# First half first in the last products, and four pieces of the memory's keys and values beside the norms

## The chip, the cores and the metric

The kernel runs on one core of a Trainium2 chip. The metric is device time in microseconds for one launch: the median of three runs, each of which carries out the whole computation once. A separate execution was recorded by the hardware profiler, and all rows of a trace come from it.

## What is computed

Two layers of a decoder trunk, 256 tokens of 1024 values, all float32. The two places that matter here are the norms and the cross-attention to a memory that does not depend on x:

```python
def layer(x, mem_n, l):                       # cut from the reference
    p = rmsnorm(x, norm_mix[l]) @ w_in[l]     # one projection, columns for four mixers
    y = concat(hgrn2(p), gated_deltanet(p), rglru(p), rwkv7(p))
    x = x + y @ w_out[l]
    h = rmsnorm(x, norm_xattn[l])
    q = h @ xattn_wq[l]
    k = mem_n @ xattn_wk[l]                   # mem_n = rmsnorm(mem), 256 tokens
    v = mem_n @ xattn_wv[l]
    x = x + softmax(q k^T / 16) v @ xattn_wo[l]      # 4 heads
    h = rmsnorm(x, norm of the FFN)
    return x + (swiglu(h) if l == 0 else top2_of_8_experts(h))
```

A final rmsnorm ends it. The delta-rule mixers (gated DeltaNet and RWKV-7) need the inverse of unit lower triangular 64x64 blocks; HGRN2 is computed in levels of doubling block size.

## The kernel before, in words

The kernel is written engine by engine: each of SyncE (SP), TensorE (PE), ScalarE (ACT) and VectorE (DVE) has its own program, and semaphores named by strings order them.

**Weights.** All large weights come in chunks of 1 MB. `plan_chunks` writes down their order, and SP issues the loads in that order (L384) into a ring of three buffers `raw`. Load d waits until the buffer of load d-3 has been read: for an ordinary chunk that is the semaphore `w_lo`, for a piece of memory weights `kv_done`. An ordinary chunk is split in two: ScalarE copies it to `whi` in a rounded format (`ahead`, L447), VectorE subtracts and writes `wlo` (`ahead`, L871). There are three pairs of split buffers; the split of chunk n waits for `chunk_done` of chunk n-3.

**Products.** Each product with x runs in three passes, high by high, low by high, high by low. A product whose output has its columns in the partitions (w_in, w_q, gate, up) takes one chunk as 48 matmuls of 128x256 (`cm_product`, L1554). A product that is added to x (w_out, w_o, the FFN's down) is summed over its chunks in four banks of PSUM, two for the first 128 tokens and two for the second; a chunk is 24 matmuls of 128x512 (`tm_product` calls `tm_part`, L1574). `tm_phase` runs four such chunks. In every chunk before the change both halves of the tokens are worked through together, pass by pass, and the semaphore `chunk_done` is raised at the end of the chunk.

**A norm.** Behind the last chunk VectorE first splits the chunks that are due (`ahead` in `tm_add`, L909), waits for `chunk_done`, and adds the four banks to x (L858). ScalarE and VectorE then make the sums of squares and the reciprocal roots, token half by token half; VectorE writes a diagonal matrix of them (L861). TensorE's `norm(i)` (L1590) multiplies x by that diagonal, which both scales and transposes it: the **turn** of x, 16 matmuls of 128x128 in fp32, 32 instructions in the trace. ScalarE and VectorE copy the result out as high and low parts, and `first_product` (L1610) takes the first chunk of the next phase, whose k-steps follow those copies. There are five norms with such a sum before them: attention and FFN in layer 0, mixer, attention and experts in layer 1.

**Memory keys and values.** For each layer there are eight **pieces**, four of `xattn_wk` and four of `xattn_wv`, each one chunk of 1 MB and 16 fp32 matmuls straight from `raw` (32 instructions, helper line L1539), in one bank (`KV_BANK`). They depend on nothing but the memory and are used at the attention alone, so they are laid between the small matmuls of the mixers. `kv(l, i, ks)` (L1614) runs the k-steps `ks` of piece i, two matmuls for each of eight k-steps; when all eight are done it raises `kv_done`, and ScalarE's `kv_put` (L486) copies the bank to `kT` or `vA` and raises `kv_put`. Before the change both layers have the same plan: pieces 0 to 3 among the levels of HGRN2 (`hgrn`, L1728), piece 4 and the two halves of piece 5 in the inverse of DeltaNet (`inverse`, L1818, called from `deltanet`, L1865), piece 6 step by step in DeltaNet's recurrence, piece 7 in `rwkv` (L1912).

**The inverse** multiplies 64x64 blocks level by level; VectorE masks each level's blocks (L858) before TensorE goes on.

## Time and profile before

| what | value |
|---|---|
| three runs | 1994.59, 1995.18, 1998.88 us |
| median | 1995.18 us |
| profiled execution | 1995.15 us, span in the trace 1993.3 us |
| TensorE busy | 1870.8 us, 94% of the span |
| VectorE busy | 1467.0 us, 74% |
| ScalarE busy | 1131.4 us, 57% |
| DMA | 465.99 MB, mean 234 GB/s |

The span is what lies between the first and the last recorded instruction; the device time holds 1.85 us more. "Busy" counts an engine's instructions that compute; a bracket such as [4.39 <-DVE TMP L861] at the end of a row gives the idle time of the engine ahead of it and what ended that. Order of the program: layer 0's mixers to 308 us, its attention to 384, its FFN to 581, layer 1's mixers to 878, its attention to about 954, then the experts. PEclk is the clock granted to TensorE as a share of the full 2.4 GHz, so 0.50 is 1.2 GHz.

### The profile page before, as it was taken

The numbers are of one execution on the slowest core, as the hardware profiler recorded it, in microseconds if no ns is written. First come the engines' busy times: TensorE is split into PE (matmuls) and PEld (weight loads), VectorE is DVE, ScalarE is ACT, GpSimd is POOL, SyncE is SP. The second block draws the span as 40 slices with busy tenths as digits, with TensorE's granted clock in tenths as the row PEclk, the third lists the DMA queues.
The fourth block names the chain that finished last, engine by engine and source line by source line (L and its number), as shares of the span: only waits on it lengthen the run. The fifth ranks groups of instructions, "written<-read, shape, count | busy, mean of one in ns | idle before, by whom it ended". The sixth has DMA issues, their size and how long they took to land.

```text
span 1993.3 us, 29711 instructions
## 1 busy us (share of the span) xinstructions
PE 1870.8 (94%) x12520; PEld 1614.1 (81%) x12521; DVE 1467.0 (74%) x1547; ACT 1131.4 (57%) x1065; POOL 0.2 (0%) x4
## 2 busy tenths in 40 slices
PE   7998799899999988899699999999999999999996
PEld 6976688799989877778588888888888888888885
DVE  6767645444457676554688989989899898998985
ACT  5555224443344652144377767777677777777774
POOL 0000000000000000000000000000000000000000
PEclk9998899999999999899899999999999999999998
DMA  7541004255545421023499999989999999999992
GB/s 238 170 148 61 27 23 162 85 188 182 183 146 169 157 78 44 23 85 106 171 334 345 379 345 366 369 335 380 341 371 365 332 382 343 371 365 335 370 377 99
DMA packets 239450, 465.99 MB, mean 234 GB/s; under 512 B 11856, under 2 KB 87760, under 8 KB 239312
## 3 DMA queue, kind: packets, MB, share of 16 engines
q1 hardware_dynamic: 239312, 464.03, 65.6%
q8 instruction: 101, 1.65, 0.3%
q14 instruction: 37, 0.30, 0.0%
HBM read 462.95 MB, written 1.05 MB: 233 GB/s over the span
## 4 chain that ended last, share of the span: by engine, by line
PE 85%; DVE 9%; ACT 3%; issue 2%; DMA 1%; DVEq 0%; SPq 0%; ACTq 0%
PE ps L2062 31%; PE ps L1554 15%; PE ps L2072 15%; PE ps L1539 11%; PE ps L1574 7%; DVE MT L858 4%; PE ps L2118 1%; ACT MT L438 1%; PE ps L2093 1%; PE ps L1610 1%; DVE MT L861 1%; PE ps L2133 1%; DVE MT L864 1%; DVE TMP L858 1%; ACT TMP L438 1%
## 5 line engine op out<-in xcount | busy, mean ns | idle before, releaser
L1315 DVE TENSOR_TENSOR wlo<-raw,whi 128x2048 fp32r<-128x2048 f32 x140 | 320.4, 2291 | 55.8 <-ACT whi L736 55.5
L736 ACT ACTIVATE whi<-raw 128x2048 fp32r<-128x2048 f32 x140 | 268.9, 1922 | 120.9 <-PE ps L2072 71.3
L871 DVE TENSOR_TENSOR wlo<-raw,whi 128x2048 fp32r<-128x2048 f32 x85 | 194.5, 2289 | 98.9 <-ACT whi L447 98.8
L1315 DVE TENSOR_TENSOR wlo<-PT,whi 128x2048 fp32r<-128x2048 f32 x84 | 192.1, 2291 | 31.3 <-ACT whi L736 30.1
L447 ACT ACTIVATE whi<-raw 128x2048 fp32r<-128x2048 f32 x85 | 162.1, 1907 | 45.3 <-PE ps L1574 43.6
L2062 PE MATMUL ps<-whi,hE_hi 128*128 128x512 f32 x672 | 185.4, 398 | 2.4 <-DVE hE_lo L1384 2.4
L736 ACT ACTIVATE whi<-PT 128x2048 fp32r<-128x2048 f32 x84 | 161.4, 1922 | 35.0 <-PE ps L2062 34.2
L2062 PE MATMUL ps<-wlo,hE_hi 128*128 128x512 f32 x672 | 180.1, 390 | 0.0
L2062 PE MATMUL ps<-whi,hE_lo 128*128 128x512 f32 x672 | 179.8, 389 | 0.0
L2062 PEld LDWEIGHTS ps<-wlo,hE_hi 128*128 128x128 f32 x672 | 126.2, 188 | 27.2
L2062 PEld LDWEIGHTS ps<-whi,hE_lo 128*128 128x128 f32 x672 | 126.1, 188 | 26.7
L2062 PEld LDWEIGHTS ps<-whi,hE_hi 128*128 128x128 f32 x672 | 122.0, 188 | 24.8 <-DVE hE_lo L1384 2.6
L2072 PE MATMUL ps<-whi,act_hi 128*128 128x512 f32 x336 | 130.8, 389 | 1.4 <-DVE act_lo L1359 1.4
L2072 PE MATMUL ps<-whi,act_lo 128*128 128x512 f32 x336 | 130.8, 389 | 0.0
L2072 PE MATMUL ps<-wlo,act_hi 128*128 128x512 f32 x336 | 130.7, 389 | 0.0
L1539 PE MATMUL ps<-MT 64*64 64x64 f32 (+1 forms) x2528 | 99.3, 233 | 26.5 <-DVE MT L858 19.2
L1539 PEld LDWEIGHTS ps<-MT 64*64 64x64 f32 (+1 forms) x2528 | 90.6, 145 | 38.7 <-issue 19.4
L1554 PE MATMUL ps<-hT_hi,whi 128*128 128x256 f32 x848 | 119.7, 284 | 0.0
L1554 PE MATMUL ps<-hT_hi,wlo 128*128 128x256 f32 x848 | 119.0, 283 | 0.0
L1554 PE MATMUL ps<-hT_lo,whi 128*128 128x256 f32 x848 | 119.0, 283 | 0.0
L858 DVE TENSOR_TENSOR MT<-MT,ps 128x256 f32<-128x256 f32 (+2 forms) x99 | 44.6, 450 | 90.0 <-PE ps L1554 75.5
L1554 PEld LDWEIGHTS ps<-hT_hi,whi 128*128 128x128 f32 x848 | 109.9, 192 | 0.9
(272 smaller groups left out, 3391.1 us busy)
## 6 DMA issues: line engine op xcount, KB each, us to landing
raw<-in_moe_w_up SPq DMA_DIRECT2D x111, 1024.0 KB, 7.2
PT<-in_moe_w_down SPq DMA_DIRECT2D x56, 1024.0 KB, 6.6
PT<-in_moe_w_gate SPq DMA_DIRECT2D x55, 1024.0 KB, 6.9
TMP<-in_moe_w_gate SPq DMA_DIRECT2D x55, 1024.0 KB, 7.0
raw<-in_moe_w_down SPq DMA_DIRECT2D x55, 1024.0 KB, 6.3
raw<-in_w_in SPq DMA_DIRECT2D x28, 1024.0 KB, 5.4
raw<-in_ffn_w_gate SPq DMA_DIRECT2D x11, 1024.0 KB, 5.4
raw<-in_ffn_w_up SPq DMA_DIRECT2D x11, 1024.0 KB, 5.5
```

The lines of the kernel that those rows point to most:

```text
L438: return chain.link(lambda: nc.scalar.activation(o, i, f, **kw))
L447: nc.scalar.activation(whi[i % SPL][:, :], raw[d % RAW][:, :], ACT.Copy).then_inc(S("w_hi"), 1)
L736: nc.scalar.activation(ex_hi[m % XSPL], ex_raw[m % XRAW], ACT.Copy).then_inc(S("w_hi"), 1)
L858: return chain.link(lambda: V.tensor_tensor(o, x0, x1, op))
L861: return chain.link(lambda: V.tensor_scalar(o, x0, s1, s2, op0, op1) if op1 else V.tensor_scalar(o, x0, s1, None, op0))
L871: V.tensor_tensor(wlo[i % SPL][:, :], raw[d % RAW][:, :], whi[i % SPL][:, :].bitcast(F32), ALU.subtract).then_inc(S("w_lo"), 1)
L1315: V.tensor_tensor(ex_lo[m % XSPL], ex_raw[m % XRAW], ex_hi[m % XSPL].bitcast(F32), ALU.subtract).then_inc(S("w_lo"), 1)
L1539: return Signalled(pe.matmul(o, lhsT, rhs, start=start, stop=stop, skip_group_check=True))
L1554: ins = pe.matmul(ps[:, bank, SEQ * m:SEQ * m + SEQ], wp[a_][:, k, P * m:P * m + P], src[b_][:, k, :], start=i == 0 and k == 0, stop=last)
L1574: ins = pe.matmul(ps[:, 4 + 2 * t + hf, :], src(b_, kk, t), wp[a_][:, kk, 512 * hf:512 * hf + 512], start=first and kk == 0 and i == 0, st ...
L2062: ins = pe.matmul(ps[:, bank, :], h_[b_][:, X_K * i + k, :], wp[a_][:, k, :], start=i == 0 and n_ == 0 and k == 0, stop=i == 1 and n_ == 2 ...
L2072: ins = pe.matmul(ps[:, 4 + hf, :], act_[b_][:, P * (TM_ROWS * i + kk):P * (TM_ROWS * i + kk) + P], wp[a_][:, kk, 512 * hf:512 * hf + 512] ...
```

## The change

Two things are done.

**The last output chunk** of w_out, w_o and down is worked through by a new function `tm_last`: all 12 matmuls for the first 128 tokens, semaphore `tm_half`, then the 12 for the second, `chunk_done`. VectorE's `tm_add` waits for `tm_half` ahead of the two sums of the first tokens, and for `chunk_done` ahead of the other two. It is used at all five places.

**Four pieces move to norms.** With PRE = 3, six matmuls of a piece (three k-steps) stand ahead of the turn and the other ten behind it. The pieces are: piece 7 of layer 0 at the attention norm of layer 0; piece 0 of layer 1 (now a piece of `xattn_wv`) at the FFN norm; piece 1 of layer 1 (`xattn_wk`) at layer 1's mixer norm; piece 7 of layer 1 at its attention norm. What was piece 5 leaves the inverse in both layers, and the later ones move up by one. In the levels of layer 1 only two pieces are left, one ahead of them and one in quarters in four levels. The loads stand in SP's queue where the pieces stand, and ScalarE's copies move with them.

```diff
+PIECES = [[("xattn_wk", j) for j in range(4)] + [("xattn_wv", j) for j in range(4)],
+          [("xattn_wv", 0)] + [("xattn_wk", j) for j in range(4)] + [("xattn_wv", j) for j in range(1, 4)]]
...
+        if layer:
+            out += pieces[1][1:2]
         out += [("cm", "w_in", layer, c) for c in W_IN_COLS]
         out += [("tm", "w_out", layer, TM_ROWS * j) for j in range(3)]
-        out += [("kv", "xattn_wk", layer, c) for c in range(0, D, CM_COLS)]
-        out += [("kv", "xattn_wv", layer, c) for c in range(0, D, CM_COLS)]
+        out += pieces[layer][2 * layer:7]
         out += [("tm", "w_out", layer, 3 * TM_ROWS)]
+        out += pieces[layer][7:]
         out += [("cm", "xattn_wq", layer, c) for c in range(0, D, CM_COLS)]
         out += [("tm", "xattn_wo", layer, r) for r in range(0, KT, TM_ROWS)]
         if layer == 0:
+            out += pieces[1][:1]
...
-        KV_BANK = [7, 5, 6, 7, 6, 7, 7, 2]
+        KV_BANK = [[7, 5, 6, 7, 6, 7, 2, 1], [3, 1, 7, 7, 6, 7, 2, 3]]
+        PRE = 3
...
-            def tm_add(n0, count, ahead_to):
+            def tm_add(k, n0, count, ahead_to):
                 ahead(ahead_to)
-                dve.wait_ge(S("chunk_done"), n0 + count)
                 for t in range(TT):
+                    if t:
+                        dve.wait_ge(S("chunk_done"), n0 + count)
+                    else:
+                        dve.wait_ge(S("tm_half"), k)
                     for hf in range(2):
...
+            def tm_last(n, src):
+                pe.wait_ge(S("w_lo"), n + 1)
+                for t in range(TT):
+                    for kk in range(TM_ROWS):
+                        ins = tm_part(n, src, False, True, kk, t)
+                    ins.then_inc(S("chunk_done" if t else "tm_half"), 1)
...
                     if v == 1:
                         pe.wait_ge(S("gd_gd"), l + 1)
+                    if l:
+                        if v == 2:
+                            pe.wait_ge(S("kv_put"), 2 * NH + 3)
+                        if 2 <= v < LEVELS - 1:
+                            kv(1, 3, range(2 * v - 4, 2 * v - 2))
+                        continue
...
-                    if v == 0:
-                        pe.wait_ge(S("y_put"), 4 * l + 2)
-                    if v < 2:
-                        kv(l, 5, range(KT // 2 * v, KT // 2 * v + KT // 2))
...
             def attention(l):
+                kv(l, 7, range(PRE))
                 pe.wait_ge(S("x_done"), 6 * l + 2)
                 norm(2 + 3 * l)
+                kv(l, 7, range(PRE, KT))
...
             def swiglu():
+                kv(1, 0, range(PRE))
                 pe.wait_ge(S("x_done"), 4)
                 norm(3)
+                kv(1, 0, range(PRE, KT))
...
             for l in range(DEPTH):
+                if l:
+                    kv(1, 1, range(PRE))
                 norm(norm_index(l))
+                if l:
+                    kv(1, 1, range(PRE, KT))
                 cm_phase(first_chunk["w_in", l], 14, norm_index(l), lambda j: gates_ahead(l, j))
```

Three places show how instructions move. (A row is a line of the code, the operation, output<-input, the tile and a count; line numbers of the changed kernel differ.) The first is TensorE at the attention norm of layer 0. Before:

```order
L1574 MATMUL ps<-wlo,hT_hi 128x512
L1574 MATMUL ps<-whi,hT_lo 128x512
L1539 MATMUL ps<-TMP,x 128x128 x16
L1610 MATMUL ps<-hT_hi,whi 128x256 x16
L1610 MATMUL ps<-hT_hi,wlo 128x256 x16
L1610 MATMUL ps<-hT_lo,whi 128x256 x16
L1554 MATMUL ps<-hT_hi,whi 128x256 x8
```

Changed:

```order
L1589 MATMUL ps<-whi,hT_lo 128x512
L1554 MATMUL ps<-raw,memT 128x256 x6
L1554 MATMUL ps<-TMP,x 128x128 x16
L1554 MATMUL ps<-raw,memT 128x256 x10
L1634 MATMUL ps<-hT_hi,whi 128x256 x16
L1634 MATMUL ps<-hT_hi,wlo 128x256 x16
L1634 MATMUL ps<-hT_lo,whi 128x256 x16
L1569 MATMUL ps<-hT_hi,whi 128x256 x8
```

The turn (`ps<-TMP,x`) has six matmuls of a piece ahead of it and ten behind it, where it stood between the two products.

The second is SP's queue from the end of the FFN to layer 1, with what each load waits for. Before:

```order
L384 DMA raw<-in_ffn_w_gate 128x8x256 [waits w_lo]
L384 DMA raw<-in_ffn_w_up 128x8x256 [waits w_lo]
L384 DMA raw<-in_ffn_w_down 128x2x1024 [waits w_lo] x2
L384 DMA raw<-in_w_in 128x8x256 [waits w_lo] x14
L384 DMA raw<-in_w_out 128x2x1024 [waits w_lo]
```

Changed:

```order
L393 DMA raw<-in_ffn_w_up 128x8x256 [waits w_lo]
L393 DMA raw<-in_ffn_w_down 128x2x1024 [waits w_lo] x2
L393 DMA raw<-in_xattn_wk 128x8x256 [waits w_lo]
L393 DMA raw<-in_w_in 128x8x256 [waits w_lo] x2
L393 DMA raw<-in_w_in 128x8x256 [waits kv_done]
L393 DMA raw<-in_w_in 128x8x256 [waits w_lo] x11
L393 DMA raw<-in_w_out 128x2x1024 [waits w_lo]
```

A piece stands ahead of the first w_in chunk, so each w_in chunk takes the buffer that is released one load later than before: the second waits for the split of the last FFN chunk, and the third for the piece to be done.

The third is TensorE in DeltaNet's inverse in layer 0 (`MT` is the blocks, `PT` and `con` the operands of RWKV's preparation between them). Before:

```order
L1539 MATMUL ps<-PT 128x128 x8
L1539 MATMUL ps<-raw,memT 128x256 x16
L1539 MATMUL ps<-con,MT 64x64 x16
L1539 MATMUL ps<-raw,memT 128x256 x8
L1539 MATMUL ps<-MT 64x64 x48
L1539 MATMUL ps<-PT,con 128x512
L1539 MATMUL ps<-raw,memT 128x256 x8
```

Changed:

```order
L1554 MATMUL ps<-PT 128x128 x8
L1554 MATMUL ps<-raw,memT 128x256 x16
L1554 MATMUL ps<-con,MT 64x64 x16
L1554 MATMUL ps<-MT 64x64 x48
L1554 MATMUL ps<-PT,con 128x512
L1554 MATMUL ps<-MT 64x64 x208
```

Both groups of eight piece matmuls are gone from it; the whole piece ahead of it stays.

## Rows read from the trace of the kernel before

**Rows 1.** Page, header: span
```profile
span 1993.3 us, 29711 instructions
```

**Rows 2.** Windows: stretch, PE PEld DVE ACT POOL busy (count), PEclk, DMA share, GB/s
```profile
696.00:722.90 26.90, 26.90 (x309) 21.98 (x310) 23.13 (x48) 9.98 (x18) 0.00 (x0) 1.00 0.36 118
985.00:1993.00 1008.00, 987.12 (x4587) 820.59 (x4585) 880.14 (x601) 718.03 (x531) 0.00 (x0) 0.99 0.94 344
```

**Rows 3.** Timeline, PE, layer 1, around the attention norm
```profile
877.87 0.39 PE L1574 MATMUL ps<-whi,hT_lo 128*128 128x512 f32 x1
...
882.65 6.05 PE L1539 MATMUL ps<-TMP,x 128*128 128x128 f32 x32 [4.39 <-DVE TMP L861]
...
895.28 0.99 PE L1554 MATMUL ps<-hT_hi,whi 128*128 128x256 f32 x7
```

**Rows 4.** Timeline, DVE, the same place
```profile
866.36 2.29 DVE L871 TENSOR_TENSOR wlo<-raw,whi 128x2048 fp32r<-128x2048 f32 x1
...
874.87 2.29 DVE L871 TENSOR_TENSOR wlo<-raw,whi 128x2048 fp32r<-128x2048 f32 x1 [3.14 <-ACT whi L447]
878.30 2.85 DVE L858 TENSOR_TENSOR x<-x,ps 128x512 f32<-128x512 f32 x4 [1.14 <-PE ps L1574]
...
881.25 0.15 DVE L861 TENSOR_SCALAR st<-st 128x1 f32<-128x1 f32 x1
```

**Rows 5.** Timeline, PE, last product's last matmul and second product's start, three other norms
```profile
307.73 0.39 PE L1574 MATMUL ps<-whi,hT_lo 128*128 128x512 f32 x1
...
324.85 1.12 PE L1554 MATMUL ps<-hT_hi,whi 128*128 128x256 f32 x8
...
383.71 0.39 PE L1574 MATMUL ps<-whi,hT_lo 128*128 128x512 f32 x1
...
400.16 1.12 PE L1554 MATMUL ps<-hT_hi,whi 128*128 128x256 f32 x8
...
580.93 0.39 PE L1574 MATMUL ps<-whi,act_lo 128*128 128x512 f32 x1
...
597.95 1.09 PE L1635 MATMUL ps<-hT_hi,wsm_hi 128*8 128x256 f32 x8
```

**Rows 6.** Chain of waits: norm, product and memory piece at full clock
```profile
417.60 5.47 PE ps L1574 x24
...
600.90 5.75 PE ps L1554 x48
...
1054.13 3.57 PE ps L2118 x32
```

**Rows 7.** Timeline, PE, one memory piece
```profile
742.15 7.17 PE L1539 MATMUL ps<-raw,memT 128*128 128x256 f32 x32
```

**Rows 8.** Windows at 1 us, start of two norms: PEclk is the third number from the end
```profile
312.00:313.00 1.00, 0.50 (x2) 0.53 (x3) 0.75 (x4) 0.95 (x4) 0.00 (x0) 0.50 0.96 398
388.00:389.00 1.00, 0.51 (x4) 0.55 (x5) 0.76 (x4) 0.95 (x4) 0.00 (x0) 1.00 0.00 0
```

**Rows 9.** Timeline, DVE, inverse's third level in layer 0 and in layer 1
```profile
196.08 0.95 DVE L858 TENSOR_TENSOR MT<-ps,con16b 128x256 f32<-128x256 f32 x2 [2.33 <-PE ps L1539]
...
764.07 0.95 DVE L858 TENSOR_TENSOR MT<-ps,con16b 128x256 f32<-128x256 f32 x2 [0.82 <-PE ps L1539]
```

**Rows 10.** DMA issues: queue, count, size, median us from issue to landing
```profile
raw<-in_w_in SPq DMA_DIRECT2D x28, 1024.0 KB, 5.4
...
raw<-in_xattn_wq SPq DMA_DIRECT2D x8, 1024.0 KB, 5.1
```

**Rows 11.** Timeline, split of the last FFN chunk (DVE) and of the second w_in chunk
```profile
571.11 2.28 DVE L871 TENSOR_TENSOR wlo<-raw,whi 128x2048 fp32r<-128x2048 f32 x1
...
575.98 1.92 ACT L447 ACTIVATE whi<-raw 128x2048 fp32r<-128x2048 f32 x1 [0.89 <-PE ps L1574]
```

**Rows 12.** Timeline, PE: an idle time of 2.71 us and the clock behind it
```profile
115.06 0.66 PE L1542 MATMUL ps<-con,PT 128*128 128x128 f32 x4 [2.71 <-ACT MT L438]
```

**Rows 13.** Windows, the same place
```profile
115.97:119.20 3.23, 3.23 (x9) 2.56 (x8) 0.00 (x0) 3.01 (x9) 0.00 (x0) 0.50 0.89 308
```

More of the change, by code:

```diff
@@ L498, in gates_ahead @@
                     mem_norm(j)
+                if l and j == 1:
+                    kv_put(1, 1)
                 if j == 6:
@@ L583, in hgrn @@
                         a(tmp(1), ps[:, 4, :], ACT.Copy).then_inc(S("hg_v"), 1)
-                    if v % 2 == 0 and v < LEVELS - 1:
-                        kv_put(l, v // 2)
+                    if v % 2 == 0 and v < LEVELS - 1 - 4 * l:
+                        kv_put(l, v // 2 + 2 * l)
                     rglru(l, v)
@@ L659, in deltanet @@
                 head_rms(l, 1, 0)
-                kv_put(l, 6)
+                kv_put(l, 5)
             def rwkv(l):
@@ L1523, in _ @@
                 split_small(l + 1)
-                tm_add(first_chunk["w_out", l], 4, first_chunk["xattn_wq", l] + 2)
+                tm_add(3 * l + 1, first_chunk["w_out", l], 4, first_chunk["xattn_wq", l] + 2)
                 attention(l)
@@ L1584, in tm_product @@
                 ins.then_inc(S("chunk_done"), 1)
+            def tm_last(n, src):
[4 more added lines that the diff above has]
+                    ins.then_inc(S("chunk_done" if t else "tm_half"), 1)
             def tm_phase(n0, src, done=0):
-                for j in range(done, 4):
-                    tm_product(n0 + j, lambda b_, kk, t: src[b_][:, TM_ROWS * j + kk, P * t:P * t + P], j == 0, j == 3)
+                for j in range(done, 3):
+                    tm_product(n0 + j, lambda b_, kk, t: src[b_][:, TM_ROWS * j + kk, P * t:P * t + P], j == 0, False)
+                tm_last(n0 + 3, lambda b_, kk, t: src[b_][:, TM_ROWS * 3 + kk, P * t:P * t + P])
             def norm(i):
@@ L1649, in gates_ahead @@
                     small_product(7, l).then_inc(S("ab_mm"), 1)
+                if l and j == 3:
+                    pe.wait_ge(S("kv_put"), 2 * NH + 2)
                 if j == 2:
@@ L1737, in hgrn @@
                 pe.wait_ge(S("sm_ready"), 2 * (l + 1))
-                kv(l, 0, range(KT))
+                kv(l, 2 * l, range(KT))
                 pe.wait_ge(S("s_kA"), l + 1)
@@ L1746, in hgrn @@
                 mm(ps[:, 6, 8:16], ones, g8).then_inc(S("gd_cum"), 1)
-                kv(l, 1, range(KT // 2))
+                if l == 0:
+                    kv(0, 1, range(KT // 2))
                 for v in range(LEVELS):
```

71 lines of the change are left out of this document (39 added, 32 removed).

## The prediction

> **What bounds the kernel now.** I first read the header of the page, a span of 1993.3 us [rows 1]. The windows then split it. From 985 us on the experts run for 1008 us with TensorE busy 987.12 us [rows 2]; the change touches nothing there, so everything is decided in the first 985 us, where TensorE waits at few places. One kind is the turn of x at each norm. In layer 1 the last output product's last matmul ends at 877.87 + 0.39 = 878.26, TensorE idles 4.39 us for the sums, the statistics and the diagonal that VectorE and ScalarE make, the turn takes 6.05 us, and the first product is done when the second starts, at 895.28 [rows 3]: 17.02 us from the last product's end. The same stretch is 324.85 - 308.12 = 16.73 us at the attention norm of layer 0, 400.16 - 384.10 = 16.06 us at the FFN norm and 597.95 - 581.32 = 16.63 us at the mixer norm of layer 1 [rows 5]. The other kind is the mixers, chains of small matmuls and VectorE work. In the chunkwise levels of layer 1 TensorE is busy 26.90 us of 26.90, but VectorE is busy 23.13 us in 48 instructions there [rows 2], and the whole idle time of 3.77 us is at most 0.08 us an instruction plus one larger stall: both engines are full, and a piece taken from TensorE alone shows up only where VectorE really waited.
>
> My base is the profiled execution, 1995.15 us (its span and 1.85 us around it). The median of the three runs is 1995.18, so the two agree.
>
> **Part 1, pieces leave the mixers.** A piece is 16 matmuls, 32 TensorE instructions, 7.17 us at full clock [rows 7], 0.224 us an instruction; four pieces are 28.7 us. In both layers the two halves of piece 5 leave the delta rule's inverse. Behind the first half VectorE has no wait; behind the second it stood 2.33 us in layer 0 and 0.82 us in layer 1 for TensorE, ahead of the third level's mask [rows 9]. The blocks that it waits for then need only X, which VectorE itself had just made, so I take back 2.3 and 0.8 us: **-3.1 us**. In the levels of layer 1 two pieces' worth leaves (16 of the 24 steps). Bounds: nothing, if VectorE carries those levels, and 3.8 us, if all its idle time were due to TensorE [rows 2]. I take 0, since 3.77 us over 48 instructions is what dependent instructions leave between them.
>
> **Part 2, the sums start earlier.** The last output chunk now does all 12 matmuls of its first 128 tokens first. A chunk is 24 matmuls in 5.47 us [rows 6], so the first half is ready 5.47 / 2 = 2.7 us before the second. But VectorE splits the next phase's second chunk just ahead of the sums: that split began at 874.87 and ended at 877.16, 1.1 us before the product's end [rows 4]. So the sums start at most 1.1 us earlier where that split stays where it is. From the start of the sums to the turn it is 4.35 us (878.30 to 882.65) [rows 3, 4]: 2.85 for four sums, then the statistics of the first tokens, from 881.25 to the turn, 1.4 us. At the experts' norm the code leaves no chunk to split ahead of the sums; there the first pair of sums is done before the product ends, and the second pair, half of 2.85 = 1.43 us, still waits for its end. The turn starts 1.43 + 1.4 + 0.1 for handing over = 2.9 us behind the product instead of 4.39: **-1.5 us**, passed on whole, since the router is a chain.
>
> **Part 3, a piece enters each of four turns.** Six matmuls (12 x 0.224 = 2.7 us) run before the turn, in idle time, ten (4.5 us) behind it. Three things pay. The idle time hides the six. A turn at full clock costs 3.57 us, as 32 matmuls of the same shape do in the experts, not 6.05 [rows 3, 6]: the clock stood at 0.50 (1.2 GHz) when the attention turn of layer 0 began and at 1.00 (2.4 GHz) when the FFN turn began [rows 8], each after 4.4 us of idle time. And the first product runs without stalls, 5.75 us [rows 6], because the high and low parts that it waited for are written under the ten. So a stretch is now (start of the turn) + 3.57 + 4.5 + 5.75 = start + 13.8 us. The start hangs on the loads. SP's queue is in order and a ring of three buffers is shared, so a piece put into the queue moves the loads behind it by one release:
> - FFN norm: the two chunks split before the sums are loaded in time; the sums start 1.1 us ahead of the product's end, the turn 3.25 us behind it. 3.25 + 13.8 = 17.05 against 16.06: **+1.0 us**.
> - Attention norms: the second w_q chunk now takes the buffer that the last w_out chunk frees at 866.36 + 2.29 = 868.65 [rows 4]. With 5.1 us to land [rows 10] it is there at 873.75, copied (1.92) at 875.7 and subtracted (2.29) at 878.0, 0.26 us before the product's end. Turn at +4.1: 17.9 against 17.02 and 16.73: **+0.9 and +1.2 us**.
> - Mixer norm of layer 1: the second w_in chunk waits for the split of the last FFN chunk, which ends at 571.11 + 2.28 = 573.39; so far it had landed before ScalarE wanted it at 575.98 [rows 11]. With 5.1 us it lands at 578.5, is copied at 580.4 and subtracted at 582.7, 1.4 us behind the product's end. The sums, behind it on VectorE, start later than now although they wait for less: turn at +5.8, 19.6 against 16.63: **+3.0 us**. The landing is 5.1 us in one row and 5.4 in the other, which gives +3.0 to +3.3.
>
> At this last turn TensorE idles 5.8 - 2.7 = 3.1 us behind the six matmuls. An idle time of 2.71 us was followed by a clock of 0.50 for 3.2 us [rows 12, 13]. I take the clock to fall here too. Bounds: 0 if it holds, 6.05 - 3.57 = 2.5 us for a whole turn at half clock; the fall comes some time after the idle time began, so **+2.0 us**.
>
> The Trainium skill, "DMA: Bandwidth & Descriptors", sections "Anatomy of one DMA" and "Where 436 GB/s comes from", gives about 2.0 us of fixed cost and 436 GB/s. For 1 MB that is an estimate of 4.4 us instead of the 5.1 measured; with it the second chunks of the two attention norms and of the mixer norm would be there 0.7 us earlier each, and the sum below would be 2.1 us smaller. The trace has the duration, so it decides.
>
> **What costs nothing.** The late loads behind a piece (third w_q, w_in or gate chunk, released when the piece is done) land some 5 us after it, about as the first product ends, and are wanted a product (5.75 us) later: 2 us of slack are left after the split. ScalarE's four copies of pieces (0.6 us each) move to places where it waits for TensorE. The banks that the pieces use are wanted only two or three products later. If this cover went, each late chunk would cost its lateness, 1 us or so.
>
> **Sum.** -3.1 - 1.5 + 1.0 + 0.9 + 1.2 + 3.0 + 2.0 = +3.5 us: 1995.15 + 3.5 = **1998.6 us**. About 0.2% (4 us) is what a measurement of this kernel can tell from no change; the forecast lies inside it, near its slow edge (1999.2).
>
> **The rivals.**
> - *The clock falls at the attention turns and in the inverses too (slower).* TensorE idles 4.1 - 2.7 = 1.4 us in those turns, and in the inverses it loses 7.2 us of work each. If the clock falls behind idle time that short too, two turns cost 2.5 us more each: 1998.6 + 5.0 = 2003.6. It decides from where the clock has fallen before the turn begins. Against it: the falls in my rows stand behind 2.7 us [rows 12, 13] and 4.4 us [rows 3, 8] of idle time. With the late loads each a little later it also covers the upper part of the range. Chance of this and of like losses that reach over 1999.2: 0.29.
> - *The clock holds at the mixer turn (same).* The FFN turn began at 1.00 after 4.4 us of idle time [rows 8], so a wait of that length does not always bring the clock down. 1998.6 - 2.0 = 1996.6; if it holds at the experts' turn as well, up to 2.5 us less: 1994.1. Chance 0.22. The Trainium skill, "TensorE: Matmul & The Clock Gate", section "HAM oscillation", says that a wait between groups of matmuls sends the next group to the slow clock. By that rule alone the fall is sure; rows 8 show that it is not at every wait of this length.
> - *The change does what its parts promise (faster).* If the loads land before they are wanted, the sums start 2.7 us early at all turns, the turn at +2.9: 2.9 + 13.8 = 16.7 in each, which is +0.6, 0, +0.1 and -0.3 instead of +1.0, +1.2, +3.0 and +0.9, and no clock falls: 1998.6 - 5.7 - 2.0 = 1990.9. Against it stands the split ahead of the sums [rows 4], which no load can move. Together with the 3.8 us of the levels it would be 1987. Chance, with a part of that gain alone counted in: 0.15.
> - The forecast itself, with its own spread of 2 us: 0.34.
>
> **The numbers.** The forecast and the second rival lie within 0.2% (0.55, which leaves 0.01 of the forecast's spread above it). Slower by over 0.2%: 0.29 + 0.01 = 0.30. Faster: 0.15. The range leaves out about 1 in 10 on each side: from 1991.5, close above the promise, to 2002.8, just short of the first rival.
>
> **What would show it.** In the changed kernel's timeline the turn of layer 1's mixer norm starts 5 to 6 us behind the last product, with the sums released by the split of the second w_in chunk, not by TensorE; the attention turns start at about +4.1, the FFN turn at +3.25, the experts' at +2.9; 32 turn instructions take 3.6 us at three turns; VectorE's wait ahead of the inverse's third level is gone, while the stretch of the levels in layer 1 is as long as before. I am wrong if the mixer turn starts at +3, if the levels of layer 1 are shorter by over 1 us, or if the clock is 0.50 in the attention turns.

## The result and the profile after

The changed kernel takes 2002.20 us (median of 7 runs, 2000.60 to 2002.73), the kernel before 1996.35 (7 runs, 1994.59 to 1998.88): ratio 1.0029, 95% interval 1.0020 to 1.0038, so 5.9 us or 0.29% slower. The forecast was 1998.6 us with a range of 1991.5 to 2002.8. The forecast added 3.5 us to its base and 5.9 us were measured; the range held the time. The likeliest case (within 0.2%, chance 0.55) did not come, the smaller one (slower by over 0.2%, chance 0.30) did.

The header and part 1 of the changed kernel's page. The profiled execution took 2000.60 us:

```profile
span 1998.8 us, 29714 instructions
...
PE 1870.5 (94%) x12520; PEld 1615.1 (81%) x12521; DVE 1466.9 (73%) x1547; ACT 1131.5 (57%) x1065; POOL 0.2 (0%) x4
```

5.5 us more span at the same busy time: what was lost is idle time or clock. The five norms in the timeline of TensorE: for each the last matmul of the last product and the turn, and at four of them the first matmuls of the second product:

```profile
306.39 0.39 PE L1589 MATMUL ps<-whi,hT_lo 128*128 128x512 f32 x1
...
310.85 3.81 PE L1554 MATMUL ps<-TMP,x 128*128 128x128 f32 x32 [1.48 <-DVE TMP L873]
...
324.56 1.12 PE L1569 MATMUL ps<-hT_hi,whi 128*128 128x256 f32 x8
...
383.43 0.39 PE L1589 MATMUL ps<-whi,hT_lo 128*128 128x512 f32 x1
...
387.05 3.81 PE L1554 MATMUL ps<-TMP,x 128*128 128x128 f32 x32 [0.64 <-DVE TMP L873]
...
400.76 1.12 PE L1569 MATMUL ps<-hT_hi,whi 128*128 128x256 f32 x8
...
581.55 0.39 PE L1589 MATMUL ps<-whi,act_lo 128*128 128x512 f32 x1
...
587.78 5.47 PE L1554 MATMUL ps<-TMP,x 128*128 128x128 f32 x32 [3.26 <-DVE TMP L873]
...
603.15 1.08 PE L1659 MATMUL ps<-hT_hi,wsm_hi 128*8 128x256 f32 x8
...
881.06 0.39 PE L1589 MATMUL ps<-whi,hT_lo 128*128 128x512 f32 x1
...
885.52 3.81 PE L1554 MATMUL ps<-TMP,x 128*128 128x128 f32 x32 [1.48 <-DVE TMP L873]
...
899.23 1.12 PE L1569 MATMUL ps<-hT_hi,whi 128*128 128x256 f32 x8
...
958.10 0.39 PE L1589 MATMUL ps<-whi,hT_lo 128*128 128x512 f32 x1
961.43 5.29 PE L1554 MATMUL ps<-TMP,x 128*128 128x128 f32 x32 [2.94 <-DVE TMP L873]
```

They answer to [rows 3, 5]. From the last product's end to the second product:

| norm | before, us | changed, us | turn begins behind the product | forecast of the turn and of the change |
|---|---|---|---|---|
| attention, layer 0 | 16.73 | 17.78 | +4.07 | +4.1, +1.2 us |
| FFN | 16.06 | 16.94 | +3.23 | +3.25, +1.0 us |
| mixer, layer 1 | 16.63 | 21.21 | +5.84 | +5.8, +3.0 and +2.0 us |
| attention, layer 1 | 17.02 | 17.78 | +4.07 | +4.1, +0.9 us |
| experts (to the router's first matmul) | 9.58 | 7.99 | +2.94 | +2.9, -1.5 us |

That is 5.7 us more than before, where the forecast had 6.6. Which load makes the mixer's turn late stands in ScalarE's timeline of the changed kernel (columns as above; the bracket names what it waited for):

```profile
579.30 1.92 ACT L456 ACTIVATE whi<-raw 128x2048 fp32r<-128x2048 f32 x1 [3.60 <-DMA raw<-in_w_in]
```

and in VectorE's, the split of the same chunk and the sums behind it:

```profile
581.25 2.29 DVE L883 TENSOR_TENSOR wlo<-raw,whi 128x2048 fp32r<-128x2048 f32 x1 [3.22 <-ACT whi L456]
583.46 2.91 DVE L870 TENSOR_TENSOR x<-x,ps 128x512 f32<-128x512 f32 x4
```

The copy waited 3.60 us for a w_in chunk, whose load SP issued at 574.04, 5.3 us before the copy began. The split ended at 583.54 (forecast 582.7; the last FFN chunk and the product ran 0.6 us later than before), 1.6 us behind the product's end at 581.94, and the sums came after it. In [rows 11] the same copy started at 575.98, as soon as ScalarE was free.

The last product of each phase ends at these times, before and after: 308.12 and 306.78; 384.10 and 383.82; 581.32 and 581.94; 878.26 and 881.45; 954.51 and 958.49. So the changed kernel was 1.3 us ahead behind the mixers of layer 0, lost 4.6 us at layer 1's mixer norm (and 0.8 to 1.1 us at three others), won 2.0 us in the mixers of layer 1, and entered the experts' norm 4.0 us late. There it won 1.6 us by its earlier turn, and yet its end is 5.5 us late. The 3.1 us in between lie in the experts' start. TensorE before, the matmuls that gather the first expert's tokens, the first of the expert's own products and a later group:

```profile
983.96 4.88 PE L2118 MATMUL ps<-MT,PT 128*128 128x128 f32 x32
...
991.23 1.19 PE L2062 MATMUL ps<-whi,hE_hi 128*128 128x512 f32 x4 [2.39 <-DVE hE_lo L1384]
...
1003.27 0.66 PE L2093 MATMUL ps<-con,MT 128*128 128x128 f32 x4 [0.85 <-DVE MT L1355]
```

and in the changed kernel:

```profile
986.34 6.36 PE L2156 MATMUL ps<-MT,PT 128*128 128x128 f32 x32
...
995.10 1.95 PE L2100 MATMUL ps<-whi,hE_hi 128*128 128x512 f32 x4 [2.39 <-DVE hE_lo L1399]
...
1008.71 0.66 PE L2131 MATMUL ps<-con,MT 128*128 128x128 f32 x4 [0.85 <-DVE MT L1370]
```

The same 32 matmuls take 6.36 us instead of 4.88, the four behind the same wait of 2.39 us 1.95 instead of 1.19, and a lag of 2.4 us behind the kernel before has become 5.4. Windows there (columns as in [rows 2]: the third number from the end is the granted clock), before and changed:

```profile
985.00:999.00 14.00, 11.61 (x63) 10.09 (x62) 7.40 (x19) 4.26 (x10) 0.00 (x0) 0.95 0.58 204
986.00:987.00 1.00, 1.00 (x10) 1.00 (x9) 0.38 (x1) 0.00 (x0) 0.00 (x0) 0.83 0.89 342
```

```profile
700.00:711.00 11.00, 3.86 (x111) 3.05 (x114) 9.49 (x23) 4.97 (x8) 0.00 (x0) 0.73 0.28 97
985.00:999.00 14.00, 10.72 (x44) 9.74 (x45) 9.57 (x27) 2.28 (x8) 0.00 (x0) 0.63 0.52 158
991.00:992.00 1.00, 1.00 (x8) 1.00 (x7) 0.83 (x4) 0.14 (x1) 0.00 (x0) 0.58 1.02 422
996.00:997.00 1.00, 1.00 (x4) 0.81 (x3) 1.00 (x1) 0.00 (x0) 0.00 (x0) 0.50 0.00 0
```

Before, the clock rose from 0.50 (1.2 GHz) to 1.00 (2.4 GHz) within the window of 986 to 987 us; in the changed kernel it rose within that of 991 to 992, and stood at 0.50 once more at 996 to 997. Of the 3.1 us, 1.5 us lie between the start of the gathering matmuls and the expert's first product, where the clock came back late, and 1.6 us behind it, where it fell a second time. The window of 700 to 711 us is among the levels of layer 1: mean clock 0.73, where [rows 2] had 1.00.

### The profile page after: what moved, and what is told of

Read it like the earlier page. It is cut to its first block, busy times and chain, and to the rows that moved or that the text cites. A ratio compares the mean times of both kernels' runs of the same rounds, so it can differ in the third digit from the quotient of the medians.

```text
span 1998.8 us, 29714 instructions
## 1 busy us (share of the span) xinstructions
PE 1870.5 (94%) x12520; PEld 1615.1 (81%) x12521; DVE 1466.9 (73%) x1547; ACT 1131.5 (57%) x1065; POOL 0.2 (0%) x4
## 3 DMA queue, kind: packets, MB, share of 16 engines
HBM read 462.95 MB, written 1.05 MB: 232 GB/s over the span
## 4 chain that ended last, share of the span: by engine, by line
PE 82%; DVE 11%; ACT 3%; issue 2%; DMA 1%; DVEq 0%; SPq 0%; ACTq 0%
PE ps L2100 31%; PE ps L1569 15%; PE ps L2110 15%; PE ps L1554 10%; PE ps L1589 5%; DVE MT L870 4%; PE ps L2156 2%; PE ps L2131 1%; PE ps L1634 1%; ACT MT L447 1%; DVE TMP L870 1%; DVE MT L873 1%; DMA raw<-in_w_in 1%; ACT TMP L447 1%; PE ps L2171 1%
## 5 line engine op out<-in xcount | busy, mean ns | idle before, releaser
L1569 PEld LDWEIGHTS ps<-hT_lo,whi 128*128 128x128 f32 x848 | 109.4, 192 | 0.0
```

Of the source, the lines that this page charges most:

```text
L1569: ins = pe.matmul(ps[:, bank, SEQ * m:SEQ * m + SEQ], wp[a_][:, k, P * m:P * m + P], src[b_][:, k, :], start=i == 0 and k == 0, stop=last)
```

## The experiments

Three questions were open: what the parts are worth each, whether the late load and the clock make the mixer norm what it is, and where the mixers' gain went. All kernels are compared with the kernel before, whose median was 1996.16 to 1996.69 us beside these runs; a ratio stands with its 95% interval. The diffs are excerpts. "Site" is the stretch from a last product's end to the second product.

**1. The half order alone.** The kernel before with `tm_last` and the wait on `tm_half`, and no piece moved:

```diff
+                for t in range(TT):
+                    for kk in range(TM_ROWS):
+                        ins = tm_part(n, src, False, True, kk, t)
+                    ins.then_inc(S("chunk_done" if t else "tm_half"), 1)
```

> The kernel before with the order of the last output chunk alone (first 128 tokens first), no piece moved. My account of the norms: the sums start 1.1 us ahead of the product's end at four norms, where VectorE's split ends 1.1 us ahead of it, so each of the four turns starts at +3.3 instead of +4.4 us and the second product 1.1 us earlier; the experts' turn starts at +2.9. Together 4 x 1.1 + 1.5 = 5.9 us less than before, 1990.5 us. Rival: the idle time that is left, 3.3 us, changes what clock the turns get; then single turns differ by 2.5 us either way. Rival: the half is worth only what the experts' norm shows, 1.5 us.

Measured 1990.93 us, ratio 0.9970 (0.9958 to 0.9982), 5.3 us less. The turns start at +3.23, +3.23, +3.14, +3.23 and +2.95 as expected. Its five turns on TensorE:

```profile
311.99 6.72 PE L1542 MATMUL ps<-TMP,x 128*128 128x128 f32 x32 [3.23 <-DVE TMP L861]
...
387.15 6.69 PE L1542 MATMUL ps<-TMP,x 128*128 128x128 f32 x32 [3.23 <-DVE TMP L861]
...
584.09 5.47 PE L1542 MATMUL ps<-TMP,x 128*128 128x128 f32 x32 [3.15 <-DVE TMP L861]
...
879.93 5.44 PE L1542 MATMUL ps<-TMP,x 128*128 128x128 f32 x32 [3.23 <-DVE TMP L861]
...
953.83 6.66 PE L1542 MATMUL ps<-TMP,x 128*128 128x128 f32 x32 [2.95 <-DVE TMP L861]
```

The sites are 15.90, 15.86, 14.84 and 14.93 us: the gain of 1.15 us is passed on at the last two of them with 0.6 to 0.9 us on top, and eaten in part at the first two, where the whole turn ran at the slow clock, 6.7 us. So it did at the experts' norm, where the turn began 1.44 us earlier and 0.2 us were left (9.36 us to the router's first matmul instead of 9.58). The five gains are 0.8, 0.2, 1.8, 2.1 and 0.2 us, 5.1 together, where four of 1.1 and one of 1.5 were expected: the sum came out nearly right, its parts did not. The half order, one of the two parts of the change, is a gain by itself.

**2. The pieces alone.** The changed kernel with the old order of the last chunk and one wait for it:

```diff
-                        dve.wait_ge(S("tm_half"), k)
+                        dve.wait_ge(S("chunk_done"), n0 + count)
```

> The changed kernel with the last output chunk back in its old order (both halves together, sums behind the whole chunk), pieces moved as in the change. If the parts add up as in my account: FFN turn at +4.4 instead of +3.2, the attention turns at +4.4 instead of +4.07, the mixer turn of layer 1 unchanged at +5.8 because the late split sets it, the experts' turn at +4.4: 1.2 + 2 x 0.3 + 0 + 1.5 = 3.3 us more than the changed kernel, 2005.5 us. Rival: the mixer turn is set by the product's end too; then it moves as the others, 4 us and more in all.

Measured 2005.23 us, ratio 1.0046 (1.0032 to 1.0060), as the parts added up (2005.5 expected). The turns start at +4.38 or +4.39 at four norms and +5.69 at the mixer's: the late split sets that one whatever the product does. The pieces alone cost 9.0 us.

**3. The loads.** The changed kernel; at both attention norms and at layer 1's mixer norm the piece's load stands behind the second chunk (the excerpt shows the mixer norm's; w_q is changed the same way):

```diff
-        if layer:
-            out += pieces[1][1:2]
-        out += [("cm", "w_in", layer, c) for c in W_IN_COLS]
+        w = [("cm", "w_in", layer, c) for c in W_IN_COLS]
+        out += w[:2] + (pieces[1][1:2] if layer else []) + w[2:]
```

> The changed kernel with the loads of three pieces one place later in the queue each than two chunks: behind the second w_q or w_in chunk (both attention norms and the mixer norm of layer 1), so that the piece and not the second chunk takes the buffer that comes free last. If the late second chunk sets the turn: mixer turn at +3.2 instead of +5.84, at full clock, 21.2 down to 17.0 us, -4.2 us; attention turns +3.2 instead of +4.07, -0.8 us each; sum -5.9 us, 1996.3 us, about the kernel before. Rival: the pieces themselves are late then, or the turn is late for the extra matmuls; then the mixer norm stays over 20 us and the time within 1 us of the changed kernel's 2002.2.

Measured 1991.90 us, ratio 0.9984 (0.9974 to 0.9994): 10.3 us under the changed kernel, and faster than the kernel before. VectorE at the mixer norm, where the product ends at 583.21:

```profile
579.82 2.29 DVE L882 TENSOR_TENSOR wlo<-raw,whi 128x2048 fp32r<-128x2048 f32 x1 [0.51 <-ACT whi L455]
582.03 2.91 DVE L869 TENSOR_TENSOR x<-x,ps 128x512 f32<-128x512 f32 x4
```

and TensorE's turn there:

```profile
586.35 3.84 PE L1553 MATMUL ps<-TMP,x 128*128 128x128 f32 x32 [0.55 <-DVE TMP L872]
...
958.14 3.81 PE L1553 MATMUL ps<-TMP,x 128*128 128x128 f32 x32 [2.95 <-DVE TMP L872]
```

(The second row is the experts' turn.) The split now ends 1.1 us ahead of the product's end, TensorE idles 0.55 us, and the turn runs at full clock. The sites are 16.94, 16.94, 16.88 and 16.95 us, worth 6.0 us together, as worked out. The other 4.4 us were not expected, and no run shows that the load order is their cause: the experts' turn took 3.81 us instead of 5.29, and the clock came back earlier in the router and did not fall a second time, so that the stretch from the last product's end to the group at 1008.71 above was 45.65 us instead of 50.22. The turn of experiment 1 stood behind the same 2.95 us of idle time and took 6.66 us. (The spans of the two profiled executions differ by 7.9 us, not 10.3, since layer 0's mixers took 2.1 us more in this one. Nine of its eleven runs took 1990.6 to 1992.7 us, two 1998.0 and 1998.6.)

**4. More of a piece ahead of the turn.** The changed kernel with `PRE = 5`:

```diff
-        PRE = 3
+        PRE = 5
```

> The changed kernel with ten matmuls of each piece ahead of the turn and six behind it, instead of six and ten. At the mixer norm the turn stays at +5.84 but TensorE idles 1.4 us ahead of it instead of 3.26. If the idle time brings the clock down, the turn there takes 3.8 us, not 5.5, and the site is 1.8 + 1.6 us shorter. The attention sites: turn at +4.6, 1.3 us shorter each; FFN 0.4 us shorter. Sum -6.4 us, 1995.8 us, less what the first product waits for the high and low parts, up to 0.5 us a site. Rival: the clock at that turn falls whatever the idle time; then -3 to -4.8 us.

Measured 1992.89 us, ratio 0.9983 (0.9974 to 0.9992), 9.3 us under the changed kernel. The mixer's turn, with the same late split:

```profile
587.00 3.84 PE L1554 MATMUL ps<-TMP,x 128*128 128x128 f32 x32 [1.62 <-DVE TMP L873]
```

It starts no earlier (+5.94), but after 1.62 us of idle time it takes 3.84 us where after 3.26 us it took 5.47. The site is 17.96 instead of 21.21 us. The four sites are 7.2 us shorter together than in the changed kernel, and the experts' turn took 1.5 us longer. The 3.5 us that the medians have beyond this are not located: the profiled execution took 1998.14 us, well above the median, and its mixers, which are the same, took 1.7 us more in layer 0 and 4.2 us more in layer 1 than in the changed kernel's profile.

**5. Both repairs.**

```diff
+        out += w[:2] + (pieces[1][1:2] if layer else []) + w[2:]
...
-        PRE = 3
+        PRE = 5
```

> Both repairs at once: the loads behind the second chunk and ten matmuls of each piece ahead of the turn. TensorE then has no idle time at four norms and the second product starts at +16.06 everywhere, 0.85 us less than with the loads alone (16.94, 16.94, 16.88, 16.95): 1991.9 - 3.4 = 1988.5 us. Rival: the repairs overlap more than that, since the load order alone gave 10.3 us of which only 6 were worked out; then 1990 to 1992.

Measured 1990.97 us, ratio 0.9979 (0.9970 to 0.9988): 0.9 us below the loads alone, so the rival held. The sites are all 16.07 us as expected, 3.4 us less, and in the profiled execution the experts' norm and router took 2.1 us more, with a turn of 5.44 us for 3.81. That the medians differ by 0.9 us and not by 1.3 or more is within their spread.

**6. Piece 5 taken out of the inverses.** The kernel before; seven of its eight k-steps are not computed:

```diff
-                    if v < 2:
-                        kv(l, 5, range(KT // 2 * v, KT // 2 * v + KT // 2))
+                    if v == 1:
+                        kv(l, 5, [KT - 1])
```

> The kernel before, but seven of the eight k-steps of piece 5 are not computed in either layer, so that the inverse holds 2 matmuls of it instead of 16 (the memory's values lose these products). Prediction's part 1: VectorE waited 2.33 and 0.82 us for the second half, so 3.1 us come back: 1993.1 us against 1996.2. Rival, from the four kernels with the change's mixers, whose first 308 us were 306.8, 311.3, 308.9 and 308.5 against 308.1 and 308.8 with the old ones: the clock falls where the piece is missing and takes it back; then within 1 us of the kernel before.

Measured 1994.45 us, ratio 0.9993 (0.9984 to 1.0002), 1.7 us less by the medians, and zero is not excluded. The mixers of layer 0 before and here:

```profile
150.00:308.00 158.00, 136.09 (x1692) 113.44 (x1691) 94.19 (x175) 52.20 (x80) 0.00 (x0) 0.92 0.15 48
```

```profile
150.00:308.00 158.00, 133.08 (x1662) 111.31 (x1662) 94.18 (x175) 52.20 (x80) 0.00 (x0) 0.90 0.15 48
```

TensorE had 28 instructions less to do, 6.3 us at full clock, but was busy only 3.0 us less: its mean clock fell from 0.92 to 0.90. VectorE's wait of 2.33 us became one of 0.59 us, a wait of 1.31 us came up 14 us ahead of it, and the third level's mask began 0.5 us earlier, not 2.3; the phase did not end earlier (308.12 and 308.64). In layer 1 the wait of 0.82 us is gone and the mask came 0.65 us earlier. The fall of the clock around the inverse is no accident of one profile: from 170 to 200 us it was 0.92 to 0.99 in the seven kernels that have piece 5 there (before and experiments 1, 7 to 11) and 0.82 to 0.87 in the seven that do not.

**7. Two pieces taken out of the levels of layer 1.** The kernel before; fourteen k-steps are not computed:

```diff
-                kv(l, 1, range(KT // 2))
+                if l == 0:
+                    kv(l, 1, range(KT // 2))
...
+                    if l:
+                        if v < 2:
+                            kv(1, 1 + v, [KT - 1])
+                        elif v < LEVELS - 1:
+                            kv(1, 3, range(2 * v - 4, 2 * v - 2))
+                        continue
```

> The kernel before, but in layer 1 fourteen of the sixteen k-steps of pieces 1 and 2 are not computed among the levels (the last layer's memory keys lose these products), as many as the change takes away there but for one. Prediction: 0, since VectorE carries the levels. Rival: up to 3.8 us less, VectorE's whole idle time. Second rival: the granted clock falls to 0.50 in the levels, as the changed kernel's trace shows for 10 us from 705 us on; the time of the levels then stays as VectorE sets it, or grows by a us or two where TensorE's matmuls are on the path.

Measured 1995.67 us, ratio 1.0000 (0.9991 to 1.0009). 700 to 711 us before and here:

```profile
700.00:711.00 11.00, 11.00 (x138) 9.20 (x138) 9.91 (x20) 3.71 (x6) 0.00 (x0) 1.00 0.29 97
```

```profile
700.00:711.00 11.00, 8.91 (x96) 6.33 (x87) 9.83 (x21) 4.34 (x7) 0.00 (x0) 0.54 0.68 222
```

The clock is at 0.54 instead of 1.00, and VectorE's work in the window is the same to 0.1 us (9.91 and 9.83 us). VectorE carries the levels, and half the clock is enough for TensorE there: from the mixer norm's second product to the last product, layer 1's mixers took 280.3 us in both profiles.

**8. Useless matmuls ahead of the turns.** The half-order kernel with six products of the memory by itself before each of five turns, into a free bank:

```diff
+            def warm(bank, count):
+                for i in range(count):
+                    mm(ps[:, bank, 0:SEQ], memT[:, i % KT, 0:P], memT[:, i % KT, :])
...
+                warm(3 if l else 1, 6)
                 pe.wait_ge(S("x_done"), 6 * l + 2)
                 norm(2 + 3 * l)
```

> The half-order kernel (no piece moved) with six matmuls of no use, memT by memT, ahead of each of the five turns, in idle time. If idle time of 3.2 us brings the clock down and 0.6 us does not: each turn takes 3.8 instead of 5.4 to 6.7 us, but the first product then waits for the high and low parts, so that 1 to 2 us a site are left: 4 to 8 us under 1990.9, 1983 to 1987 us. Rival: the pieces cost by their own length alone and the clock is no matter; then within 1 us of 1990.9.

Measured 1982.37 us, ratio 0.9934 (0.9921 to 0.9948): 8.6 us under the half order alone, 13.8 under the kernel before. TensorE at layer 0's attention norm, the turn and the second product:

```profile
312.92 3.81 PE L1542 MATMUL ps<-TMP,x 128*128 128x128 f32 x32 [0.64 <-DVE TMP L861]
...
322.96 1.12 PE L1557 MATMUL ps<-hT_hi,whi 128*128 128x256 f32 x8
```

The site is 13.26 us; the others are 13.27, 13.21 and 13.61. The turn costs 3.81 or 3.84 us at all five norms. This is a little below the 1983 to 1987 us expected.

**9. The same in the kernel before.** Nine useless matmuls at each norm, no `tm_last`:

```diff
+                warm(3 if l else 1, 9)
                 pe.wait_ge(S("x_done"), 6 * l + 2)
                 norm(2 + 3 * l)
```

> The kernel before with nine useless matmuls (4.1 us) ahead of each of the five turns, and nothing else. The turns stay at +4.4 but at full clock: second product at +14.4 instead of +16.1 to +17.0, 2.2 us less at four norms, 1.6 at the experts': -10 us, 1986 us; with the half order of the last chunk that is the warm kernel's 1982.4 plus 4 to 6. Rival: the fast turn only makes the first product wait for its high and low parts; then -3 to -5 us.

Measured 1988.21 us, ratio 0.9961 (0.9947 to 0.9975), 8.5 us less. The sites are 14.42, 14.43, 14.36 and 14.77 us. That is 10.1 us less with the experts' norm (7.96 for 9.58); 8.5 arrive, and the router's slow stretch is 17.1 us for 13.7. With 5.3 us of the half order the two add up to the 13.8 us of the kernel with both; by the ratios it is 7.8 and 6.0 against 13.2 us, so they add up within a microsecond.

**10. A ladder of idle times.** As 8, with 5, 4, 3, 2 and 1 useless matmuls:

```diff
-                warm(3 if l else 1, 6)
+                warm(3 if l else 1, 2 if l else 5)
```

> The warm kernel with 5, 4, 3, 2 and 1 useless matmuls at the five norms in order, so that TensorE idles 1.0, 1.4, 1.8, 2.3 and 2.5 us ahead of the turns. With the idle time as the cause, the turns after the short waits take 3.8 us and those after the long ones 5.4 us or more; in the changed kernel 1.5 us was short enough and 3.3 us was not. Rival: whether the clock falls is not set by this length; then long and short turns come in no order, as before, where 4.4 us of idle time gave a slow start at three norms and a full one for a microsecond at the FFN's.

Two runs, 1982.19 and 1986.36 us. The five turns on TensorE, each with the idle time ahead of it:

```profile
312.29 3.81 PE L1542 MATMUL ps<-TMP,x 128*128 128x128 f32 x32 [1.07 <-DVE TMP L861]
...
384.81 3.81 PE L1542 MATMUL ps<-TMP,x 128*128 128x128 f32 x32 [1.50 <-DVE TMP L861]
...
579.15 3.84 PE L1542 MATMUL ps<-TMP,x 128*128 128x128 f32 x32 [1.85 <-DVE TMP L861]
...
873.35 5.44 PE L1542 MATMUL ps<-TMP,x 128*128 128x128 f32 x32 [2.37 <-DVE TMP L861]
...
947.24 3.81 PE L1542 MATMUL ps<-TMP,x 128*128 128x128 f32 x32 [2.52 <-DVE TMP L861]
```

1.07, 1.50 and 1.85 us are followed by a fast turn, 2.37 us by a slow one, and 2.52 us by a fast one. Up to 1.85 us the clock held at every norm of every kernel here; above 2.3 us it fell at all norms but two (2.52 us here and 2.95 us in experiment 3), and when is not the same each time: from 2.1 us ahead of the turn's start (attention, layer 1, before) to 1.4 us behind it (experiment 1, same norm).

**11. The router too.** As 8, with 8, 11 and 2 useless matmuls in the router's three waits:

```diff
                 small_product(0, 2, 6).then_inc(S("rt_mm"), 1)
+                warm(3, 8)
                 small_turn(1, 2).then_inc(S("rt_mm"), 1)
+                warm(3, 11)
                 pe.wait_ge(S("rt_d"), 2)
```

> The warm kernel with 21 more matmuls of no use in the three waits of the experts' router (4.1, 5.2 and 1.1 us), where the granted clock falls to 0.50 for 13.6 to 17.1 us in every trace so far. If the clock follows idle time: the 32 transposing matmuls behind the router take 3.6 instead of 5.0 us, and no slow stretch is left behind 960 us: -2 us, 1980.4 us. Rival: the filler lies in the way of the router's own small matmuls; then 1982.4 us or more.

Measured 1981.36 us, ratio 0.9926 (0.9912 to 0.9939): 1.0 us under experiment 8, which these runs do not tell from nothing. The slow stretch of the router is gone but for 3.4 us, which fall on the gathering matmuls:

```profile
970.36 4.96 PE L2144 MATMUL ps<-MT,PT 128*128 128x128 f32 x32
```

They start after a wait of 1 us and take 4.96 us, not 3.6. Of the 2 us expected half came by the medians, and 0.3 us in the profiles (39.26 and 38.98 us from the router's first matmul to the later group).

**12. Pieces instead of useless matmuls.** Both repairs, with the useless matmuls of 11 at the experts' norm and in the router only:

```diff
+                warm(3, 6)
                 pe.wait_ge(S("x_done"), 10)
```

> The kernel with both repairs of the change (loads, ten matmuls ahead) and the useless matmuls at the experts' norm and in the router. It differs from the router-warm kernel only in that real pieces, not useless matmuls, keep TensorE busy at four norms. At each norm the second product is at +16.07 instead of +13.3: 4 x 2.8 = 11 us more; the mixers hold four pieces less and give back 0 to 4 us. So 7 to 11 us over the router-warm kernel, 1987 to 1991 us. Rival: the pieces are worth their full 28.7 us less what the norms lose; then it is the fastest of all.

Measured 1987.36 us, ratio 0.9956 (0.9942 to 0.9970): 6.0 us more than 11, a little under the 7 to 11 expected. It differs in where four pieces are, and at these four norms the pieces stand in place of the useless matmuls. The sites are 16.07 instead of 13.27, 13.26, 13.21 and 13.62, 10.9 us more; so by the medians the mixers gave back 4.9 us of the pieces' 28.7. The profiled executions show 2.0 of it (0.4 us in layer 0, 1.5 in layer 1); they differ by 9.3 us, and that of this kernel was its slowest run.

## Why the prediction was right, and where it was not

The range held the time, and the parts tell how much of that was understood. The norms came as worked out, within 0.9 us together. The mixers' term has the right size for partly other reasons. The experts' start lost 3.1 us for which the forecast has no term.

*The norms.* Part 3 held at its starts and its waits. The turns began within 0.1 us of the forecast at all five norms, released as it said, and the second products came 1.05, 0.88, 4.58 and 0.76 us later than before, against 1.2, 1.0, 5.0 and 0.9. That the late second chunk makes the mixer's turn late is shown by run 3, which moves nothing but loads and takes 4.3 us off that site; that the clock fell for its idle time, by run 4, where the turn starts as late after 1.62 us of idle time and stays fast. The turn there took 5.47 us, 1.7 us over a fast one where the forecast put 2.0. The rival in which the clock falls at the attention turns too did not occur there: 1.48 us of idle time was short enough.

*The half order.* Run 1 has 5.3 us for the 5.9 that part 2 gives alone, but by parts that differ, and that near agreement is luck. What the forecast did not count is the clock: the half order takes the idle time from 4.4 to 3.2 us (2.9 at the experts'), which does not save it, and at three of five norms the slow clock lasted through the whole turn.

*The experts' start: the step that failed.* "Passed on whole, since the router is a chain": the turn began 1.45 us earlier, the router's small matmuls 1.6, but behind the router the clock came back some 5 us later than before, where the work stood 2.4 us later, it fell once more behind the wait at 995 us, and 3.1 us were lost. The forecast has no term for this. The terms then sum up: 3.5 of the forecast, 0.9 less at the norms, 0.3 less in the mixers, 3.1 more here make 5.4, where the spans differ by 5.5 and the medians by 5.9. A chain of short matmuls and waits brings TensorE to the slow clock in every kernel that has no useless matmuls in the router. Added up over windows of 1 us, that lasts 13.6 us (13.7 before) or 17.1 us. The longer stretch by itself costs little: from the router's first matmul to the later group it is 39.18 us before, 39.4 to 39.6 us in runs 1, 2, 4, 5, 9 and 10, which all have the 17.1 us, and 42.23 us in the changed kernel, whose gathering matmuls took longest and which alone shows the second fall. So part of the 3.1 us may be this one profile. That the earlier turn is the cause of the longer stretch is not shown: with the half order it is 17.1 us in the changed kernel and runs 1, 4, 5 and 10 but 13.6 in runs 3 and 8, and it is 17.1 in runs 2 and 9, which lack it.

*The mixers: a sum that came out right by luck.* Part 1 took 3.1 us back, and the two phases were 1.3 and 2.0 us shorter in the changed profile. In layer 0 VectorE's wait of 2.33 us [rows 9] is gone:

```profile
181.38 0.42 DVE L870 TENSOR_TENSOR MT<-ps,con16b 128x256 f32<-128x256 f32 x1 [1.05 <-PE ps L1554]
...
194.75 0.95 DVE L870 TENSOR_TENSOR MT<-ps,con16b 128x256 f32<-128x256 f32 x2
```

but 13 us earlier it waits 1.05 us for TensorE where it had not waited at all, so the inverse gave 1.3 us for the 2.3 of the forecast. In layer 1 it gave 0.7 for 0.8. Most of the rest of layer 1's 2.0 us arose 70 us later, in RWKV, at eight matmuls of a piece; both kernels have a piece at that place. TensorE before, changed, and in experiment 1, whose mixers are those of the kernel before:

```profile
835.79 3.47 PE L1539 MATMUL ps<-raw,memT 128*128 128x256 f32 x8
```

```profile
840.65 1.99 PE L1554 MATMUL ps<-raw,memT 128*128 128x256 f32 x8
```

```profile
835.93 1.99 PE L1542 MATMUL ps<-raw,memT 128*128 128x256 f32 x8
```

Before, the granted clock had fallen there (0.80 over 8.4 us from 836.0 us on); in the changed kernel it held (1.00), and in experiment 1 too, without any piece having moved. So the forecast's 3.1 us stand against 2.0 us from the inverses and over 1 us of clock that fell well. Over the profiles of the six kernels with the changed mixers (changed, runs 2 to 5 and 12) layer 0's mixers ended at 308.9 us in the mean (306.8 to 311.3), over the six with the old ones (before, runs 1 and 8 to 11) at 309.4 (308.1 to 311.2); for layer 1's, from second to last product, the means are 279.5 (277.9 to 282.5) and 280.8 us (280.0 to 282.8). That is 1.9 us together, inside the spread. Run 6 measures the inverses at 1.7 us with zero not excluded. The levels were rightly put at nothing, for the right reason (run 7).

*The clock as a rival.* The Trainium skill's "TensorE: Matmul & The Clock Gate", section "HAM oscillation", was cited for the rule that waits between groups of matmuls cost the fast clock. (The page ties it to waits that are long enough, which the prediction left out.) Runs 3 and 10 show that it does not at every wait: 2.95 and 2.52 us of idle time left a turn fast. [Rows 8] do not show it, and the rival built on them read them wrongly. Its FFN turn began at 1.00 after 4.4 us of idle time, but the next window of the kernel before (columns as in [rows 2]) is:

```profile
389.00:390.00 1.00, 1.00 (x7) 1.00 (x6) 0.62 (x3) 0.92 (x1) 0.00 (x0) 0.50 0.08 16
```

The clock fell half a microsecond into that turn, which took 5.44 us and not 3.8. It fell at all five norms of the kernel before, so the chance of 0.22 for that rival rested on a wrong reading. The clock weighed more than the forecast gave it. From the last product to the second, and at the experts' norm to the router's first matmul, the kernel before needs 76.0 us at its five norms and run 8 59.9; of the 16.1 us between them 10.1 go with useless matmuls alone (run 9).

What stays open: what decides whether the clock falls after 2.4 to 3.2 us of idle time, why it comes back later in some routers, and how much of the 3.1 us at the experts' start each execution has, since one of each kernel was profiled. Also not tried was a piece kept in the mixers with useless matmuls in the inverses.

## What to carry to other kernels

Before real work is moved into idle time, ask what it costs at both ends: here a piece saved 0.3 to 1.2 us of its 7.2 in the mixers by the medians (runs 7 and 12, the first not told from nothing), where TensorE was busy but not what bounded them, and cost 2.7 us at the norm, where everything behind the turn is on the path. Where several transfers share one in-order queue, put the load of the filler behind the loads that the critical step wants. And where TensorE idles over 2 us ahead of work on the path, a few matmuls of no use there are worth more than the idle time looks like: six of them at five norms gave 8.6 us.

## What the runs showed of the hardware

- TensorE's clock fell to 0.50 behind idle times at a norm of 2.37 us (experiment 10), 2.94 (changed kernel, experiments 4 and 5), 2.95, 3.15 and 3.23 (experiment 1), 3.10 (experiment 2), 3.26 (changed kernel) and 4.3 to 4.4 us (before), and held behind 0.35 to 1.85. It also held behind 2.52 (experiment 10) and 2.95 (the experts' norm of experiment 3). The same 2.95 us were followed by a turn of 6.66 us in experiment 1 and of 3.81 in experiment 3.
- The fall can come after the work has begun: 0.5 us into the FFN turn before (window 389 to 390 us), so that the clock at a turn's start does not tell what the turn will cost. The turn's 32 matmuls take 3.7 to 3.8 us at full clock, 5.3 to 6.3 where the clock is at 0.50 for a part of them, and 6.7 to 6.8 us where it is slow throughout or nearly so.
- Useless matmuls hold it: 3.81 to 3.84 us for the turn in all ten cases of experiments 8 and 9.
- Taking work from a busy TensorE can lower its clock: from 0.92 to 0.99 down to 0.82 to 0.87 around layer 0's inverse (170 to 200 us, seven kernels each), 1.00 to 0.54 among the levels (experiment 7), at the same time for the whole.
- The same eight matmuls in layer 1's RWKV took 3.47 us before and 1.99 in experiment 1, with the same mixers, and six kernels with the changed mixers ended layer 0's between 306.8 and 311.3 us. So a gain of 2 us in one profile of these mixers says little.
